# Expert stages mixed: 64 up slabs, then steps of one up slab and two down slabs, with the coefficients as the stationary operand of the down products

## The reference, cut to what matters

```python
def peer_ffn(h, peer_wq, peer_keys, peer_u, peer_v):
    q = (ht @ peer_wq).reshape(T, PEER_HEADS, 2, PEER_DH)
    s = jnp.einsum('thpd,hpkd->thpk', q, peer_keys)
    sv, si = lax.top_k(s, PEER_TOPK)                  # 16 of 128 keys, two key sets
    ...                                               # 256 sums per head, top 16 of them
    g = jax.nn.softmax(top, axis=-1)
    u = peer_u[ib]                                    # 128 picks per token of 16384 experts
    a = jax.nn.gelu(jnp.einsum('td,thkd->thk', hb, u))
    return jnp.einsum('thk,thkd->td', gb * a, peer_v[ib])
```

## Time and profile before

| | us |
|---|---|
| median of 3 runs | 1783.68 (1782.01 to 1784.19) |
| the profiled execution | 1786.27 |
| its span in the trace | 1784.5 |
| PE busy | 1660.3 |
| PEld busy | 1510.1 |
| DVE busy | 1420.8 |
| ACT busy | 695.1 |
| POOL busy | 607.4 |
| DMA | 443.82 MB, mean 249 GB/s |

### The profile page before, as it was taken

The page is one execution under the profiler, slowest core; times in us unless marked ns, Lnnn a source line. Parts: engine busy times, 40 slices in busy tenths (PEclk is TensorE's granted clock), DMA queues, the critical chain, the costliest instruction groups (busy, mean ns, idle before and its releaser), DMA issues.

```text
span 1784.5 us, 29098 instructions
## 1 busy us (share of the span) xinstructions
PE 1660.3 (93%) x9345; PEld 1510.1 (85%) x9345; DVE 1420.8 (80%) x2563; ACT 695.1 (39%) x987; POOL 607.4 (34%) x633
## 2 busy tenths in 40 slices
PE   2899889999899996899898899899999999999998
PEld 1675447887688996798898898899999999999998
DVE  7795646657599999988898898865888888888886
ACT  4331655233434333254454454443333333333331
POOL 2100000101234554555555555541333333333331
PEclk8999789999999998899999999999999999999999
DMA  7521114655322554488898998988999999999996
GB/s 248 175 95 36 60 41 152 222 187 189 118 83 96 178 170 131 153 290 329 320 338 335 336 335 322 357 300 318 341 343 352 349 338 350 354 336 349 354 339 227
DMA packets 182381, 443.82 MB, mean 249 GB/s; under 512 B 13728, under 2 KB 95776, under 8 KB 180656
## 3 DMA queue, kind: packets, MB, share of 16 engines
q1 hardware_dynamic: 118768, 234.91, 38.4%
q0 software_dynamic: 42784, 156.26, 23.6%
q10 hardware_dynamic: 20768, 51.89, 7.8%
HBM read 388.47 MB, written 54.53 MB: 248 GB/s over the span
## 4 chain that ended last, share of the span: by engine, by line
PE 61%; DVE 24%; DMA 7%; issue 4%; ACT 3%; DVEq 0%; POOL 0%; ACTq 0%; POOLq 0%; SPq 0%
PE bank L1528 10%; PE bank L1527 10%; PE bank L1526 10%; PE bank L1278 8%; PE bank L1279 7%; PE bank L1280 7%; DMA sb_x<-u_rows_dram,sb_scr 4%; DVE sb_scr L1081 2%; DVE sb_wide L1184 2%; DVE sb_x L1145 2%; DMA a_scratch<-sb_scr 2%; PE bank L1501 2%; PE bank L1389 1%; DVE sb_scr L829 1%; DVE sb_w_lo L815 1%
## 5 line engine op out<-in xcount | busy, mean ns | idle before, releaser
L1278 PE MATMUL bank<-sb_act_hi,sb_w_hi 128*128 128x384 f32 (+1 forms) x1424 | 511.8, 359 | 14.4 <-POOL sb_w_lo L440 13.6
L1279 PE MATMUL bank<-sb_act_lo,sb_w_hi 128*128 128x384 f32 (+1 forms) x1424 | 503.1, 353 | 0.0
L1280 PE MATMUL bank<-sb_act_hi,sb_w_lo 128*128 128x384 f32 (+1 forms) x1424 | 503.0, 353 | 0.0
L497 ACT ACTIVATE sb_w_hi<-sb_stage 128x1024 fp32r<-128x1024 f32 x324 | 342.3, 1057 | 377.0 <-PE bank L1528 329.4
L815 DVE TENSOR_TENSOR sb_w_lo<-sb_stage,sb_w_hi 128x1024 fp32r<-128x1024 f32 x266 | 324.4, 1220 | 98.8 <-ACT sb_w_hi L497 92.2
L1528 PE MATMUL bank<-sb_mix_hi,sb_w_lo 128*128 128x384 f32 x1024 | 342.0, 334 | 0.0
L1527 PE MATMUL bank<-sb_mix_lo,sb_w_hi 128*128 128x384 f32 x1024 | 342.0, 334 | 0.0
L1526 PE MATMUL bank<-sb_mix_hi,sb_w_hi 128*128 128x384 f32 x1024 | 342.0, 334 | 0.0
L1278 PEld LDWEIGHTS bank<-sb_act_hi,sb_w_hi 128*128 128x128 f32 x1424 | 271.9, 191 | 36.6 <-POOL sb_w_lo L440 15.0
L1279 PEld LDWEIGHTS bank<-sb_act_lo,sb_w_hi 128*128 128x128 f32 x1424 | 271.9, 191 | 15.2 <-issue 0.5
L1280 PEld LDWEIGHTS bank<-sb_act_hi,sb_w_lo 128*128 128x128 f32 x1424 | 270.8, 190 | 15.9
(11 more groups left out here) (192 smaller groups left out, 1767.2 us busy)
## 6 DMA issues: line engine op xcount, KB each, us to landing
sb_stage<-u_dram SPq DMA_DIRECT2D x128, 512.0 KB, 3.9
sb_stage<-v_dram SPq DMA_DIRECT2D x128, 512.0 KB, 6.5
sb_stage<-w_front_dram SPq DMA_DIRECT2D x68, 512.0 KB, 3.3
a_scratch<-sb_scr ACTq DMA_DIRECT2D x128, 192.0 KB, 4.1
g_scratch<-sb_scr ACTq DMA_DIRECT2D x12, 2048.0 KB, 9.6
sb_scr<-g_scratch SPq DMA_DIRECT2D x32, 768.0 KB, 7.9
sb_scr<-a_scratch SPq DMA_DIRECT2D x32, 768.0 KB, 10.6
sb_scr<-w_ada_dram POOLq DMA_DIRECT2D x32, 512.0 KB, 4.4
```

The source lines that it names most:

```text
L497: nc.scalar.activation(w_hi[:, slot, :], stage[:, slot, :], ACT.Copy).then_inc(w_round, 1)
L1278: nc.tensor.matmul(out, w_hi[:, slot, w], rhs_hi[:, dc, :], start=(i == 0), stop=False)
L1279: nc.tensor.matmul(out, w_hi[:, slot, w], rhs_lo[:, dc, :], start=False, stop=False)
L1280: last = nc.tensor.matmul(out, w_lo[:, slot, w], rhs_hi[:, dc, :], start=False, stop=(i == len(dcs) - 1))
```

## The change

64 up slabs run first (`EARLY`), with slab 64 (`FUSED`) behind them; their activations go to HBM as before. Then follow 64 steps, four to a lap: one down slab for an old up slab (activations read back), one new up slab, and one down slab for the new slab of the step before, whose activations stay on the chip in `ga`. The last step has no new up slab. In the down products the coefficients are now stationary (128 experts x 128 tokens) and 512 columns of the weight slab stream: 18 matmuls of 512 columns in place of 24 of 384. The sums stand token by token in six banks and are copied and transposed at the end. Banks 6 and 7 take the new up slabs.

So that the gate matrix is whole before the steps, it is made beside slabs 36 to 59: 6 turns of 4 slabs, two batches a slab, no dots. Its scratch is laid out in groups of four expert slabs, so a DMA of 32 tokens writes pieces of 512 bytes, and tiles are read in pieces of 6 KB. Top-k runs for tiles 0 and 1, then their lists, then tiles 2 and 3 and their lists; the wait for `ro_ok` now stands ahead of the first top-k. Lists are transposed after slabs 14 and 16, the third in the first gate turn; exponentials are taken at slabs 9 and 34. Tile GT is the last, so all gathers come later: GpSimd splits the slabs up to number 37 without a pause, then gathers. The gather takes its index column directly (no copy), into eight row buffers. Eight dots are done beside slabs 60 to 63, the others in the steps, two dots and two additions in each. Shortened, the diff is:

```diff
-EXP_SLAB = 27
-LIST_SLABS = (32, 35, 38)
-G_FIRST = 40
-G_UNITS = 12
+EARLY = 64
+STEPS = SLABS - EARLY
+EXP_SLABS = {9: (0, 1), 34: (2, 3)}
+LIST_SLABS = (14, 16)
+G_FIRST = 36
+G_UNITS = 4
...
+        tiles = [[at((3 * s + k) * 4 * ND, [4 * ND]) for k in range(3)] for s in range(2)]
+        g_old = [tiles[s][0].rearrange("p (t b) -> p t b", b=4) for s in range(2)]
+        g_new = [tiles[s][1].rearrange("p (t b) -> p t b", b=4) for s in range(2)]
+        a_old = [tiles[s][2].rearrange("p (b t) -> p b t", b=4) for s in range(2)]
+        cf = at(9216, [2, ND])
...
+            def lap_loads(lap, s, first=False, last=False):
+                def unit_load(c, src):
+                    slot = (STEP0 + c) % RING
+                    load(lap * (3 * LAP) + (STEP0 + c), slot, src).then_inc(w_in[slot], 16)
+                for k in range(LAP):
+                    unit_load(3 * k, v_d[bass.ds(lap * LAP + k, 1)])
+                    if k == 1 and not last:
+                        old_g(lap + 1, 1 - s, first)
+                        old_a(lap + 1, 1 - s, first)
+                    if not (last and k == LAP - 1):
+                        unit_load(3 * k + 1, u_d[bass.ds(lap * LAP + (EARLY + 1 + k), 1)])
+                    if first and k == 0:
+                        for i in range(2):
+                            sp.wait_ge(gw_out[i], 16 * G_TURNS)
+                        old_g(0, 0, True)
+                        old_a(0, 0, True)
+                        new_g(0, 0, True)
+                    if k == 2 and not last:
+                        new_g(lap + 1, 1 - s, first)
+                    if k == 1 and last:
+                        sp.wait_ge(c_mul, 2 * LAP * (LAPS - 1))
+                        sp.wait_ge(x2_out, 16)
+                        sp.dma_start(xend, x2_d.rearrange("c p t -> p c t")).then_inc(x2_in, 16)
+                    unit_load(3 * k + (1 if last and k == LAP - 1 else 2), v_d[bass.ds(lap * LAP + (EARLY + k), 1)])
...
-            with pool.Fori(WQ0 // RING + 1, (FRONT + EARLY_SLAB) // RING) as turn:
+            with pool.Fori(WQ0 // RING + 1, (FRONT + G_FIRST) // RING) as turn:
                 for slot in range(RING):
                     split_unit(turn * RING + slot, slot)
+            for n in range(FRONT + G_FIRST, POOL_LAST):
+                split_unit(n, n % RING)
             pool.wait_ge(x2_out, 16)
...
+            def gather(g, which, k):
+                if g >= ROWS:
+                    pool.wait_ge(row_used, g - ROWS + 1)
+                pool.indirect_dma_start(row(g), None, v_rows_d if which else u_rows_d,
+                                        bass.IndirectOffsetOnAxis(ap=idx3[:, which, k:k + 1], axis=0)
+                                        ).then_inc(row_in[g % ROWS], 16)
...
+                for tt in EXP_SLABS.get(q, ()):
+                    act.wait_ge(tk_ok, tt + 1)
+                    v = top[:, tt, :, :].rearrange("p h k -> p (h k)")
+                    nc.scalar.activation(v, v, ACT.Exp).then_inc(te_ok, 1)
...
+                            act.dma_start(g_d[:, :, bass.ds(it * (8 * TB) + 4 * TB * s, 4 * TB)].rearrange("a p n -> p a n"),
+                                          gb[:, s, :, :, :].rearrange("p a t b -> p a (t b)")).then_inc(gw_out[s], 16)
...
+                for k in range(LAP):
+                    idx = lap * (2 * LAP) + 2 * k
+                    round_at(3 * k + 3)
+                    c_high(idx + 1, 2 * k + 1, unit(3 * k + 2))
+                    if last and k == LAP - 1:
+                        break
+                    round_at(3 * k + 4)
+                    c_high(idx + 2, 2 * k + 2, unit(3 * k + 3))
+                    round_at(3 * k + 5)
+                    if isinstance(lap, int) and lap == 0 and k == 0:
+                        act.wait_ge(a_out[1], 16 * EARLY // 2)
+                    else:
+                        act.wait_ge(c_mul, idx)
+                    gelu_new(None, (k + 1) % 2, unit(3 * k + 1))
+                if not last:
+                    gelu_dots(lap + 1, 1 - off % 2)
...
-            for h in range(PH):
-                for tt in range(TT):
-                    topk(tt, h)
...
             dve.wait_ge(ro_ok, 1)
-            for at_ in range(TT):
+            for h in range(PH):
+                for tt in range(2):
+                    topk(tt, h)
+            for tt in range(2):
+                below_top(tt)
+            for tt in range(2):
                 for part in range(3):
-                    indices(at_, (GT + at_) % TT, part)
-
-            dve.wait_ge(ht_cp, 2)
-            dve.wait_ge(ijt_cp, 3 * DT)
+                    indices(tt, part)
+            for tt in range(2, TT):
+                for h in range(PH):
+                    topk(tt, h)
+                below_top(tt)
+            for tt in range(2, TT):
+                for part in range(3):
+                    indices(tt, part)
+
...
-                    for d in share(G_DOTS, b):
-                        dot(it * (G_DOTS // 4) + d // 4, d % 4)
...
+                for k in range(LAP):
+                    idx = lap * (2 * LAP) + 2 * k
+                    split_at(3 * k + 2)
+                    new_product(idx + 1, 2 * k + 1, turns, s, k, lap * LAP + (EARLY + k + 1))
+                    take(2 * k)
+                    split_at(3 * k + 3)
+                    c_low(idx + 1, 2 * k + 1)
+                    if not (last and k == LAP - 1):
+                        if k < LAP - 1:
+                            old_product(idx + 2, 2 * k + 2, turns, s, k + 1)
+                        else:
+                            old_product(idx + 2, 2 * k + 2, turns1, 1 - s, 0)
+                    take(2 * k + 1)
+                    split_at(3 * k + 4)
+                    if not (last and k == LAP - 1):
+                        c_low(idx + 2, 2 * k + 2)
+                    if k == 0:
+                        dve.wait_ge(g8_ok, lap + 1)
+                        nc.vector.tensor_tensor(w8, w3[:, bass.ds(lap * PICKS_LAP, PICKS_LAP)], g8, ALU.mult
+                                                ).then_inc(w8_ok, 1)
+                        dve.wait_ge(w8_ok, lap + 1)
+                    add(2 * k)
+                    add(2 * k + 1)
...
+            def v_slab(n, slot, idx, c, first=False, final=False):
+                pe.wait_ge(w_split, n + 1)
+                pe.wait_ge(c_lo, idx + 1)
+                for half in range(2):
+                    w = slice(half * 512, half * 512 + 512)
+                    for tt in range(DT):
+                        out, t = bank[half * DT + tt][:, :], slice(tt * P, (tt + 1) * P)
+                        nc.tensor.matmul(out, mix_hi[:, c, t], w_hi[:, slot, w], start=first, stop=False)
+                        nc.tensor.matmul(out, mix_hi[:, c, t], w_lo[:, slot, w], start=False, stop=False)
+                        last = nc.tensor.matmul(out, mix_lo[:, c, t], w_hi[:, slot, w], start=False, stop=final)
+                        if final:
+                            last.then_inc(o_sum, 1)
+                if not final:
+                    last.then_inc(w_used, 1)
...
+            def lap_ops(j, off, first=False, last=False):
+                lap = j * 2 + off
+                for k in range(LAP):
+                    idx, n = lap * (2 * LAP) + 2 * k, lap * (3 * LAP) + (STEP0 + 3 * k)
+                    slot = (STEP0 + 3 * k) % RING
+                    v_slab(n, slot, idx, 2 * k, first=(first and k == 0))
+                    end = last and k == LAP - 1
+                    if not end:
+                        new_slab(n + 1, (slot + 1) % RING, (k + 1) % 2, lap * LAP + (EARLY + k))
+                    v_slab(n + (1 if end else 2), (slot + (1 if end else 2)) % RING, idx + 1, 2 * k + 1, final=end)
...
+            pe.wait_ge(row_used, 2 * PICKS)
             for m in range(DC):
-                nc.tensor.transpose(bank[m][:, ND:T], acc[:, m * P:(m + 1) * P], ident).then_inc(t3_ok, 1)
+                pe.wait_ge(o_cp[m // 4], DT)
+                out = bank[(m + 6) % 8]
+                for tt in range(DT):
+                    nc.tensor.transpose(out[:, tt * P:(tt + 1) * P], oend[:, tt, m * P:(m + 1) * P], ident)
+                nc.tensor.transpose(out[:, ND:T], acc[:, m * P:(m + 1) * P], ident).then_inc(t3_ok, 1)
...
```

More of the change, by code:

```diff
@@ new lines, in _ @@
+            for g in range(EARLY_DOTS):
+                if g == 4:
+                    pool.wait_ge(g_ok, ND // 4)
+                gather(g, 0, g)
+            g = EARLY_DOTS
+            for step_ in range(STEPS):
+                for which in range(2):
+                    for k in range(2):
+                        pick = 2 * step_ + k + (0 if which else EARLY_DOTS)
+                        if pick < PICKS:
+                            gather(g, which, pick)
+                            g += 1
@@ new lines, in _ @@
+            lap_ops(0, 0)
+            with act.Fori(0, LAPS // 2 - 1) as j:
+                lap_ops(j, 1)
+                lap_ops(j, 2)
```

(33 more changed lines are left out.)

420 lines of the change are left out of this document (202 added, 218 removed).

## The result

The changed kernel takes **1829.51 us** (median of 4 runs, 1826.97 to 1831.94) against 1783.32 for the kernel before: a ratio of 1.0259, 95% interval 1.0242 to 1.0277. It is slower by 46 us. Forecast were 1815 us and slower, with a range of 1793 to 1850. The profiled execution has a span of 1830.1 us; the sum of the prediction was 1815.3.

The account below looks back on a forecast made before the run. TensorE was taken to bound the down slabs, VectorE's top-k chain the stretch before the gate stage. Steps ending at 1802.4 + 8.9 + 4 gave a 1815.3 span, predicted as 1815 us; range 1793 to 1850.

Parts of the forecast that it names:

- part 4: Slabs 60 to 64 and turn to the steps: about 5 us of stall, bounds 0 and 12, reaching 1018.1.
- part 5: The steps: down slabs at 4.08 us against 4.16, a step 12.32, VectorE holds it; 784.3 us, to 1802.4.
- Part 1: VectorE's top-k and list chain: starts at 564.3 instead of 479.40, losing 84.9 us of head start; ends at 815.3.
- The rival in which splits cost nothing: VectorE's chain: GpSimd splits fall into stalls, so it ends at 781 and the total is 1781, not slower; chance 0.12.
- Part 2: Gate stage of 24 slabs instead of 72: VectorE slowest at 7.15 us per slab, 177 us taken, to 992.3.
- Part 3: Gate matrix writes in 512-byte pieces: landing between 9.6 and 21 us, near the low end; 4 us in all.
- a rival held at 0.01: Down slabs in the steps: 512 columns run at the skill page's pace of 131 ns, giving 1596; chance 0.01.
- that rival: VectorE binds in the steps as row landings slip: period 13.0, 45 us more, 1860; chance 0.10.
- Part 6: The end after the last matmul: 8.9 us against 8.5 now, VectorE operations the chain, bounds 8.5 and 12.

Follow-up runs that it names:

- the last version: Changed kernel with the ro_ok wait behind the first sixteen top-k, late gathers held, and four dots moved behind the first coefficient: 1754.20 us, ratio 0.9842.
- the swap alone: Kernel before with only the down-product operands swapped, coefficients stationary, 18 matmuls of 512 columns per down slab: 1775.01 us, ratio 0.9957.

## Why the prediction was right, and where its sizes were off

The direction and its mechanism stood: a head start of 85 us is lost, and TensorE can use only part of that time. The loss came out half as large again as forecast (46 us against 31), for one mis-sized term in part 4 and a smaller one in part 5. By the prediction's own steps:

- **Part 1, top-k.** Right in each date: first top-k 564.3 forecast, 564.2 measured; TensorE stops at 617, 616.6; slab 13 at 661, 660.7; two tiles done at 654, 654.2; second half done at 789.5, 789.0. The end of the chain, 815.3, was 814.7 (first split of the stage). ScalarE stood 50.9 us at slab 9, forecast about 55. The chain took 250.5 us against 278.8 in the kernel before; VectorE's busy time, 242.3 against 268.6, makes up nearly all of the 28 us that the prediction put down to spared collisions. So the sum built on 0.7 us per split in a top-k and 2.1 in a list, from the earlier trace rows, held; no run takes the splits away. The rival in which splits cost nothing put the end at 781.
- **Part 2, gate stage.** 7.15 us a slab forecast, 7.16 measured; slab 60 at 992.3, measured 989.99. The allowance for the restart at the lower clock, 2 us, was not used up: of the two batches that end the stall the first takes 2.74 us at a granted clock of 0.50, against 1.54 in the earlier trace rows, and from 824.1 us on the clock is 1.00 again. VectorE stays the bound. The 2.3 us won here hide a part of what part 4 lost.
- **Part 3, gate writes.** Median landing 9.1 us, at the low end of 9.6 to 21. In the stage each write held ScalarE's next issue 4.3 to 5.2 us, hidden behind VectorE: with 16 KB pieces the hold is gone and slab 60 comes no earlier (table above). The 4 us of the sum were spent, but in the turn and not in the stage. The 9.6 us of the earlier trace rows come from a stage with more traffic (DMA share 0.89 against 0.75); in the same stage as here, the 16 KB writes land in 7.4 us. By the 512-byte rule of the Trainium skill (DMA: Bandwidth & Descriptors, Specifications) the two should be alike; 9.1 against 7.4 us bears it out only roughly, and the pieces differ in where they lie as well as in size.
- **Part 4, the turn: the mis-sized term.** I took 5 us of stall, bounds 0 and 12; slab 60 to the first down product took 39.4 us, against 20.8 + 5 = 25.8. That is 13.6 too little, or 11.3 in the date (1018.1 against 1029.4). TensorE stood 6.6 and 9.4 us, and slab 64 between the two waits took 6.5 us instead of 4.16 at a granted clock of 0.65. Two assumptions failed. First, the last write was to land in 10 us. It took 20.0, to 1011.0 instead of 1004, and all that is read back came 7 us later. Second, the load of `v` slab 64, which stands behind SyncE's wait, was called covered, as TensorE needs it 8 us later. But ScalarE works in order and rounds that slab ahead of the first coefficient:

```profile
1021.26 0.84 DVE L1264 TENSOR_TENSOR sb_scr<-sb_scr 128x384 f32<-128x384 f32 x1 [2.56 <-DMA sb_scr<-a_scratch]
...
1027.19 1.06 ACT L519 ACTIVATE sb_w_hi<-sb_stage 128x1024 fp32r<-128x1024 f32 x1 [5.03 <-DMA sb_stage<-v_dram]
...
1028.15 0.51 ACT L783 ACTIVATE sb_mix_hi<-sb_scr 128x384 fp32r<-128x384 f32 x1
```

  The coefficient was multiplied at 1022.1 and its rounding began at 1028.15, 6 us later. The gap is 4.2 us with the wait moved, 5.7 with 16 KB pieces and 5.9 in the last version, each time behind ScalarE's wait for this slab. No run changed that order, so this share is read from traces and not shown by an experiment. The runs with 16 KB pieces and with held gathers took 4.8 and 5.8 us off the turn, in single executions of a turn that varies by 4 us. Moving four dots took off another 4.8, of which 3.7 stayed to the end.
- **Part 5, the steps.** 784.3 forecast, 791.3 measured (1029.4 to 1820.7). 2.7 us are the first down slab, mostly at the half clock after the 9.4 us wait (0.58 in 1029.4 to 1036.2). The rest is pitch: a step takes 12.39 us, not 12.32. The rows:

```profile
1147.70 0.33 PE L1375 MATMUL bank<-sb_act_hi,sb_w_hi 128*128 128x384 f32 x1
...
1160.09 0.33 PE L1375 MATMUL bank<-sb_act_hi,sb_w_hi 128*128 128x384 f32 x1
```

  The down slabs alone keep 4.08 us, as the swap alone shows, so the 0.07 belongs to the mixed order; that it is the change between the two shapes was not tried by itself. The Trainium skill (TensorE: Matmul & The Clock Gate, Back-to-back issue gap) gives 131 ns as the pace of 512 columns, a rival held at 0.01; it is 227 ns here. VectorE was busy 684 of 790 us, and TensorE did not wait for it again after the first down product: that rival is out. The gate read at a stride of four elements costs 845 ns, against 550 in the earlier trace rows and the 1100 allowed.
- **Part 6, the end.** 9.4 us, forecast 8.9.

The 14.8 us between 1815.3 and 1830.1: +11.3 for the date of the first down product (parts 1 to 4), +7.0 for the steps, +0.5 for the end, and -4 for the writes' own term, which lies inside the first.

In the whole, by ratios to the kernel before: the wait costs 3.65% (65 us), the swap gains 0.43% (7.7 us), and what is left of the change, the mixed order with the shorter gate stage, gains 0.63% (11 us) as a remainder, not measured alone. What the changed kernel wins by its new order it loses more than three times over at the wait that now stands ahead of the first top-k.

## What to carry to other kernels

A wait at the head of a long in-order chain costs the head start and not its own length: read when the awaited signal comes, and ask who could have run before it. Price the first turn between two stages by all that is issued in it on every queue, not by the transfer that is awaited, and look at what each in-order engine has to do ahead of the awaited step; a stage that hides a slow issue leaves it bare at its end. When a mixed change is slower, undo its smallest reordering first: here one line was worth more than the whole loss.

## What the runs showed of the hardware that was not expected

- In the gate stage a DMA of 2 MB in 512-byte pieces landed in 9.1 us (median), in 16 KB pieces in 7.4. But the next DMA issued by the same engine took 4.3 to 5.2 us, and 6.77 to 14.10 with eight gathers about, against 0.35 after 16 KB pieces.
- Eight row gathers (4 MB) beside a write in 512-byte pieces moved its landing from 8.2 to 20.0 us; beside one in 16 KB pieces it was 9.7.
- An up slab and two down slabs, mixed, take 0.07 us more than the same slabs in runs of one shape (12.39 against 4.16 + 2 x 4.08).
- The up stage began at 557.1 to 562.5 us in the ten profiled executions, and at 557.1 and 559.8 in two versions whose code is the same up to there. Single spans of this kernel are therefore not to be compared to better than some 5 us, unless they are counted from a common point such as the start of the up stage.
